# Linear attention: the last 32 low-rank rows of the gate as 96 stacked rows of one product

## The chip, the cores and the metric

The kernel runs on one core of a Trainium2 chip. The time is that of one execution on the device in microseconds; three runs of the kernel before gave 3934.86, 3940.90 and 3945.79, median 3940.9. A core has five engines with an instruction queue each: TensorE (PE, matrix products; its weight loads are listed as PEld), VectorE (DVE), ScalarE (ACT), GpSimd (POOL) and SyncE (SP, which here issues the loads). They wait for each other by semaphores alone.

## The reference

Two blocks of two layers each over 512 tokens of width 1024. The change lies in the first block, in the linear attention (an RWKV-7 time mix), and there in the gate `g`:

```python
zs = z + (shifted(z) - z) * mu
r, k, v, wd, ad, gd = split(zs, (1024, 1024, 1024, 64, 64, 160))
w = -softplus(-(w0 + tanh(wd) @ w2)) - 0.5      # decay
iclr = sigmoid(a0 + ad @ a2)                    # in-context rate
g = sigmoid(gd) @ g2                            # gate: 160 low-rank rows -> 1024
...
out = (groupnorm(scan(r, decay, k, v, ...)) + bonus) * g
```

The gate has 160 low-rank rows: a full tile of 128 and a rest of 32.

## The kernel before, in words

Activations are held transposed, channels on the partitions and 512 tokens along the columns. A product in full precision is made of three passes (`split_matmuls`, line 227): each factor is split into a high part, rounded to the format that PE takes at full rate, and a low part, what is left of it; high times high, high weight times low activation and low weight times high activation are summed in PSUM. Weights come as a stream of units, 128 rows by 1024 columns each, through two raw slots: SP loads a unit (`stream_loads`, L309), ACT writes its high part `Whi` (`HighParts`, L284), POOL its low part `Wlo` (`low_parts`, L299), both into one of three slots. PE takes unit u when the semaphore `w_lo` says that its low part is there.

The linear-attention stage first makes three low-rank tiles (decay and rate; the gate's first 128 rows; the gate's last 32 rows, the other 96 of that tile being zero), splits them into `loh` and `lol` (ACT L1327, DVE L1405), and then works through eight pairs of heads. A pair uses four units: r, k, L (all low-rank weights of the pair: decay, rate, gate 128 rows, gate rest) and v. `rwkv_lora_pe` takes unit L: six passes of 64 rows for decay and rate (L621), and the gate in two tiles of three passes each (through L232). The gate's second tile has 32 rows that count.

The order is written out by hand for each engine. For pair p, PE issues the scores (`rwkv_front_pe`, L709), then the low-rank products and the v product of pair p+1, then the five levels of a triangular inverse (`rwkv_inv_pe`, L719) with pieces of the r and k products of pair p+2 between them, then the tail (chunk states, output). The first pair's products stand before the loop. ACT evicts decay (wS, L885), rate (aS, L885) and gate (gS, L880), in that order, and then makes the high parts of the next r and k unit (L284). POOL multiplies the level masks (TM, L1146), and between the levels splits the next r and k unit in quarters of 256 columns (L299); in the tail it prepares b and k (L1099, L1101) and splits units L and v, in quarters as well. DVE masks the scores (L1124), forms the inverse's start (L1154 to L1159, the last being XT), scans the decay (L1048), mixes k (L1027, L1029, L1060: kkr) and adds up the levels (X L1166, XT L1168).

The output of pair p-1 is centred by DVE (L1216) in pair p, and the PSUM bank that its mean stands in is claimed again by PE for another product (`gv`) beside level 2 of the inverse: `claim` makes PE wait for L1216 there.

Of the kernel before, what the change touches and what calls it, by code (L numbers as in the profile page):

```python
# [18 lines left out]
F32 = mybir.dt.float32  # L19
# [6 lines left out]
ADD, SUB, MUL, MAX = ALU.add, ALU.subtract, ALU.mult, ALU.max  # L26

P = 128
# [8 lines left out]
LEAD = 2  # L37
PART = 8
GRING = 12
LOW_PIECES = 4  # L40
# [7 lines left out]
PAIRS = 8  # L48
# [178 lines left out]
def split_matmuls(pe, ps, left, right, n, start=True, stop=True):  # L227

    last = None
    for k in range(n):  # L230
        for i, (a, c) in enumerate(((0, 0), (0, 1), (1, 0))):
            last = pe.matmul(ps, left[a](k), right[c](k), start=start and k == 0 and i == 0,  # L232
                             stop=stop and k == n - 1 and i == 2)
    return last


def tiles_of(high, low):

    return (lambda k: high[:, k]), (lambda k: low[:, k])


def columns_of(unit, n, at=0, width=P, j=0, m=P):

    def part(x):
        w = x[:, at:at + n * width].rearrange("p (k n) -> p k n", k=n)
        return lambda k: w[:, k, j:j + m]
    return part(unit[0]), part(unit[1])


def weight_slot(b, u):  # L250
    return (u + b["slot0"]) % SLOTS


def raw_slot(b, u):
    return (u + b["raw0"]) % RAW
# [33 lines left out]
        self.upto(act, u + SLOTS)  # L289


def low_parts(pool, s, b, first, end, pieces=1):

    for u in range(max(first, LEAD), end):
        pool.wait_ge(s["w_hi"], u - LEAD + 1)
        slot = weight_slot(b, u)
        for i in range(pieces):
            part = slice(i * UNIT // pieces, (i + 1) * UNIT // pieces)
            last = pool.tensor_tensor(b["Wlo"][:, slot, part], b["raw"][:, raw_slot(b, u), part], b["Whi"][:, slot, part].bitcast(F32), SUB)  # L299
        last.then_inc(s["w_lo"], 1)  # L300


def stream_loads(sp, s, b, first, end, beside=None):

    for u in range(first, end):
        if u >= RAW + LEAD:
            sp.wait_ge(s["w_lo"], u - RAW - LEAD + 1)
        units, total = b["units"], b["units"].shape[0]
        sp.dma_start(b["raw"][:, raw_slot(b, u)], units[u] if u < total else b["next_units"][u - total]) \  # L309
            .then_inc(s[f"w_in{u % RAW}"], 16)  # L310
        if beside:
            beside(u)


def ada_load(sp, s, b, ada, layer, m):
# [119 lines left out]
def angle_sine(act, s, b, name, i, dst):  # L435
# [12 lines left out]
               first=("kkr", "c0", "c1", "c2", "c3", "cx", "big", "rn", "kk", "b", "kf", "ks", "na", "nr", "rk"))  # L448
# [17 lines left out]
POST_A = Steps("sq", "sd")  # L466
POST_V = Steps("d", "rr", "rw", "yn", "ya", "o", "og", "yh", "yl")

RWKV_SEMS = ["lo_hi", "lo_lo", "prep_g", "y_out", "lo_mm", "lo_z", "lo_d", "lo_mix", "lo_act", "gemm_p", "gemm_ev", "mix", "prep_v", "prep_a",
             "ssq_p", "front_p", "front_a", "front_v", "inv_g", "inv_p", "inv_a", "inv_v",  # L470
             "tail_p", "tail_a", "tail_v", "post_p", "post_a", "post_v", "bonus_p", "bonus_v"]

# [140 lines left out]
def rwkv_lora_pe(pe, s, b, ring, p):  # L613
    w = ring.take(pe)
    if p == 0:
        pe.wait_ge(s["lo_lo"], 3)
    banks = [claim(pe, s, b, "g", p, y) for y in "wa"]
    low = (b["loh"], b["lol"])
    for i, (a, c) in enumerate(((0, 0), (0, 1), (1, 0))):
        for h in range(2):  # L620
            last = pe.matmul(banks[h], w[a][half(h), h * P:(h + 1) * P], low[c][half(h), 0], start=i == 0, stop=i == 2)  # L621
            if i == 2:
                last.then_inc(s["gemm_p"], 1)
    ps = claim(pe, s, b, "g", p, "g")
    if p:
        pe.wait_ge(s["front_a"], FRONT_A(p - 1, "trV"))
    split_matmuls(pe, ps, columns_of(w, 2, at=2 * P), tiles_of(b["loh"][:, 1:3], b["lol"][:, 1:3]), 2).then_inc(s["gemm_p"], 1)


def head_sums(pe, ps, src, b):  # L630
# [239 lines left out]
def unit1(p, x):  # L870
    return 3 + 4 * p + ("rkLv" if p else "krLv").index(x)
# [523 lines left out]
def rwkv_dve(dve, s, b):  # L1395
    def mixed(i):
        dve.wait_ge(s["lo_z"], i + 1)
        dve.tensor_tensor(b["dz"][:, i], b["zp"][:, i, 0:TOK], b["zp"][:, i, 1:TOK + 1], SUB).then_inc(s["lo_d"], 1)
        dve.wait_ge(s["lo_d"], i + 1)
        dve.scalar_tensor_tensor(out=b["lo"][:, i], in0=b["dz"][:, i], scalar=b["p"]("mu", i),  # L1400
                                 in1=b["zp"][:, i, 1:TOK + 1], op0=MUL, op1=ADD).then_inc(s["lo_mix"], 1)

    def low(i):
        dve.wait_ge(s["lo_hi"], i + 1)
        dve.tensor_tensor(b["lol"][:, i], b["lo"][:, i], b["loh"][:, i].bitcast(F32), SUB).then_inc(s["lo_lo"], 1)  # L1405

    mixed(0)
    mixed(1)
    low(0)
    low(1)  # L1410
    mixed(2)
    low(2)
    rwkv_mix_dve(dve, s, b, 0, "k")
    rwkv_kk_dve(dve, s, b, 0)
    rwkv_mix_dve(dve, s, b, 0, "r")
    rwkv_scan_dve(dve, s, b, 0)
    rwkv_prep1_dve(dve, s, b, 0)
    rwkv_rn_dve(dve, s, b, 0)
    rwkv_prep2_dve(dve, s, b, 0)
    rwkv_prep3_dve(dve, s, b, 0)  # L1420
    rwkv_turned_dve(dve, s, b, 0)
    rwkv_mix_dve(dve, s, b, 0, "v")
    rwkv_prep4_dve(dve, s, b, 0)
    for p in range(PAIRS):
        rwkv_front_dve(dve, s, b, p)

        def between(l):
            if p + 1 < PAIRS and l == 0:
                rwkv_scan_dve(dve, s, b, p + 1)
                rwkv_mix_dve(dve, s, b, p + 1, "k")  # L1430
                rwkv_kk_dve(dve, s, b, p + 1)
            if l == 1 and p:
                rwkv_mean_dve(dve, s, b, p - 1)
            if p + 1 < PAIRS:
                if l == 1:
                    rwkv_prep1_dve(dve, s, b, p + 1)
                    rwkv_mix_dve(dve, s, b, p + 1, "r")
                if l == 2:
                    rwkv_mix_dve(dve, s, b, p + 1, "v")
                if l == 3:  # L1440
                    rwkv_rn_dve(dve, s, b, p + 1)
            if l == 4 and p:
                rwkv_rr_dve(dve, s, b, p - 1)
            if p + 1 < PAIRS:
                if l == 4:
                    rwkv_prep2_dve(dve, s, b, p + 1)
                if l == 5:
                    rwkv_turned_dve(dve, s, b, p + 1)
                    rwkv_prep3_dve(dve, s, b, p + 1)
            if l == 5:  # L1450
                rwkv_bonus_dve(dve, s, b, p)
        rwkv_inv_dve(dve, s, b, p, between)
        rwkv_tail_dve(dve, s, b, p)
    p = PAIRS - 1
    rwkv_mean_dve(dve, s, b, p)
    rwkv_rr_dve(dve, s, b, p)
    rwkv_out_dve(dve, s, b, p, ("yn", "ya", "o", "og", "yh", "yl"))


def rwkv_pool(pool, s, b):  # L1460
    low_parts(pool, s, b, 3, unit1(1, "L"))
    rwkv_prep_pool(pool, s, b, 0)
    low_parts(pool, s, b, unit1(1, "L"), unit1(2, "r"))
    for p in range(PAIRS):
        def between(l):
            if l in (1, 3):
                u = unit1(p + 2, "r" if l == 1 else "k")
                low_parts(pool, s, b, u, u + 1, LOW_PIECES)
            if p + 1 < PAIRS and l == 5:
                rwkv_prep_pool(pool, s, b, p + 1, "bk")  # L1470
            if l == 5:
                u = unit1(p + 2, "L")
                low_parts(pool, s, b, u, u + 2, LOW_PIECES)
        rwkv_inv_pool(pool, s, b, p, between)


# [1426 lines left out]
def ktiles(w, cols=slice(None)):  # L2903

    w = w[:, :, cols]
    return w.reshape(w.shape[0], -1, P, w.shape[2]).transpose(0, 2, 1, 3)


def rows_up(w, n=P):
    return np.concatenate([w, np.zeros((w.shape[0], n - w.shape[1], w.shape[2]), w.dtype)], 1)  # L2910


def layout1(a):
    L = LAYERS
# [5 lines left out]
    w = a["w_in"]  # L2920
    q0, k0, v0, r0, g0 = 0, 1024, 1280, 1536, 1536 + 3360
    rw = r0
    lo0 = rw + 3072
    def tile(m, c, k=slice(None)):

        return unit_of(ktiles(m, slice(c, c + P))[:, :, k])

    last = np.zeros((L, P, KD, P), np.float32)
    last[..., :32] = ktiles(w, slice(lo0 + 256, lo0 + 288))
    units = [tile(w, lo0), tile(w, lo0 + P), unit_of(last)]  # L2930
    wv = w[:, :, rw + 2048:rw + 3072][:, :, swap]
    g2 = a["rw_g2"][:, :, swap]
# [1 line left out]
    for p in range(PAIRS):  # L2934
        c = slice(p * P, p * P + P)
        of = {"r": tile(w, rw + p * P), "k": tile(w, rw + 1024 + p * P),
              "L": unit_of(np.concatenate([a["rw_w2"][:, :, c], none], 1), np.concatenate([none, a["rw_a2"][:, :, c]], 1),
                           g2[:, :P, c], rows_up(g2[:, P:, c])), "v": tile(wv, p * P)}
        units += [of[x] for x in ("rkLv" if p else "krLv")]
    wq = w[:, :, q0:q0 + 1024][:, :, qperm]  # L2940
    units += [tile(wq, P * i) for i in range(8)] + [tile(w, k0), tile(w, k0 + P), *[unit_of(ktiles(w, slice(v0, v0 + 256))[:, :, k:k + 4]) for k in (0, 4)]]
# [14 lines left out]
    stream = np.ascontiguousarray(np.stack(units, 1))  # L2956

    mu = a["rw_mu"]
    mu_lo = np.concatenate([mu[:, 3072:3360], np.zeros((L, 96), np.float32)], 1)
    mu_all = np.concatenate([mu_lo, mu[:, :2048], mu[:, 2048:3072][:, swap]], 1)  # L2960
    sink = a["att_sinks"][:, order].reshape(L, 8, 1, 2)
    sink = np.broadcast_to(sink, (L, 8, BLK, 2)).reshape(L, 1, 64)
# [208 lines left out]
```

## Time and profile before

| what | value |
|---|---|
| runs of the kernel before | 3934.86, 3940.90, 3945.79 us, median 3940.9 |
| profiled execution | span 3931.4 us from first to last instruction; the page gives no time around it |
| mean granted clock of PE | 0.979 |
| PE busy | 3743.9 us, 95% of the span, 30890 products |
| DVE, ACT, POOL busy | 1848.1, 1581.7, 1779.5 us |
| linear-attention stage | from the first low-rank tile at 39 us to the last output at 462 us in layer 1; the last output of layer 2 at 1721 us |

The page's busy time of PE counts each product from its start to its modelled end, and products overlap; what a product costs is read from the starts of those that follow each other. The list of waits says how long an engine stood still before a group of instructions, and for whom. The timeline gives start, duration, engine, line, operation, operands and, in brackets, the idle time before it and its releaser. Where several instructions of a line follow each other they are merged into one row (x4).

### The profile page before, as it was taken

The numbers are of one execution on the slowest core, as the hardware profiler recorded it, in microseconds if no ns is written. First come the engines' busy times: TensorE is split into PE (matmuls) and PEld (weight loads), VectorE is DVE, ScalarE is ACT, GpSimd is POOL, SyncE is SP. The second block draws the span as 40 slices with busy tenths as digits, with TensorE's granted clock in tenths as the row PEclk, the third lists the DMA queues.
The fourth block names the chain that finished last, engine by engine and source line by source line (L and its number), as shares of the span: only waits on it lengthen the run. The fifth ranks groups of instructions, "written<-read, shape, count | busy, mean of one in ns | idle before, by whom it ended". The sixth has DMA issues, their size and how long they took to land. (4 is left out here: it accounts for less than half of the span.)

```text
span 3931.4 us, 72626 instructions
## 1 busy us (share of the span) xinstructions
PE 3743.9 (95%) x30890; PEld 3040.7 (77%) x30904; DVE 1848.1 (47%) x2868; ACT 1581.7 (40%) x2643; POOL 1779.5 (45%) x1132
## 2 busy tenths in 40 slices
PE   7999989999998999998999999899999999999998
PEld 6777758878887777776887887677878877787887
DVE  7777652155635877754226553543231133423112
ACT  5555352343334555535234333454332234433222
POOL 5555444434445555544443444463444435344443
PEclk9999999989998999999998999899999999999999
DMA  4111203335532211122334553212222221222322
GB/s 142 52 56 56 88 28 135 99 134 193 183 107 76 92 51 56 56 99 72 99 105 143 189 182 104 69 65 76 97 86 97 97 85 66 70 96 87 97 97 86
DMA packets 108753, 379.88 MB, mean 97 GB/s; under 512 B 12560, under 2 KB 12944, under 8 KB 107792
## 3 DMA queue, kind: packets, MB, share of 16 engines
q1 hardware_dynamic: 102816, 365.66, 27.8%
q10 hardware_dynamic: 5616, 9.58, 0.7%
q8 instruction: 246, 4.03, 0.4%
q14 instruction: 75, 0.61, 0.1%
HBM read 359.46 MB, written 15.73 MB: 95 GB/s over the span
## 5 line engine op out<-in xcount | busy, mean ns | idle before, releaser
L299 POOL TENSOR_TENSOR Wlo<-raw,Whi 128x1024 fp32r<-128x1024 f32 (+1 forms) x744 | 1385.8, 1876 | 1671.6 <-ACT Whi L284 1671.4
L232 PE MATMUL ps<-hh,Whi 128*128 128x512 f32 x2864 | 1150.9, 402 | 22.1 <-DVE hl L383 10.1
L232 PE MATMUL ps<-hl,Whi 128*128 128x512 f32 x2864 | 1125.3, 393 | 0.0
L232 PE MATMUL ps<-hh,Wlo 128*128 128x512 f32 x2864 | 1124.4, 393 | 0.1
L284 ACT ACTIVATE Whi<-raw 128x1024 fp32r<-128x1024 f32 x552 | 578.7, 1054 | 689.3 <-PE ps L232 617.8
L232 PEld LDWEIGHTS ps<-hh,Whi 128*128 128x128 f32 x2864 | 543.3, 190 | 147.8 <-issue 15.7
L232 PEld LDWEIGHTS ps<-hh,Wlo 128*128 128x128 f32 x2864 | 543.0, 190 | 116.2 <-issue 0.5
L232 PEld LDWEIGHTS ps<-hl,Whi 128*128 128x128 f32 x2864 | 543.8, 190 | 108.1 <-issue 1.9
L232 PE MATMUL ps<-gh,Whi 128*128 128x512 f32 x864 | 337.9, 391 | 3.8 <-POOL Wlo L299 3.8
L232 PE MATMUL ps<-gh,Wlo 128*128 128x512 f32 x864 | 336.5, 390 | 0.0
L232 PE MATMUL ps<-gl,Whi 128*128 128x512 f32 x864 | 336.5, 389 | 0.0
L1146 POOL TENSOR_TENSOR TM<-TD,const 128x256 f32<-128x256 f32 x192 | 157.4, 843 | 152.3 <-PE ps L719 75.7
L1799 DVE TENSOR_TENSOR sg<-sg,ps 128x512 f32<-128x512 f32 x64 | 44.0, 688 | 366.9 <-PE ps L232 366.6
L232 PEld LDWEIGHTS ps<-gh,Whi 128*128 128x128 f32 x864 | 162.2, 188 | 39.0 <-POOL Wlo L299 5.5
L232 PEld LDWEIGHTS ps<-gh,Wlo 128*128 128x128 f32 x864 | 162.2, 188 | 33.8
L232 PEld LDWEIGHTS ps<-gl,Whi 128*128 128x128 f32 x864 | 162.3, 188 | 33.2
L2736 DVE SCALAR_TENSOR_TENSOR xT<-ps,mod,xT 128x512 f32<-128x512 f32 x64 | 48.1, 752 | 281.7 <-PE ps L232 281.7
L1992 ACT ACTIVATE acc<-ps,par 128x512 f32<-128x512 f32 x88 | 68.6, 780 | 273.5 <-PE ps L232 273.5
L2726 DVE TENSOR_TENSOR gt<-gt 128x512 f32<-128x512 f32 x64 | 47.9, 749 | 256.8 <-ACT gt L2614 256.8
L2043 DVE SCALAR_TENSOR_TENSOR acc<-ps,par,acc 128x511 f32<-128x511 f32 x88 | 66.0, 750 | 197.7 <-ACT acc L1992 197.7
L1782 ACT ACTIVATE sg<-ps 128x512 f32<-128x512 f32 x64 | 38.3, 599 | 239.2 <-PE ps L232 239.2
L719 PEld LDWEIGHTS ps<-X,TM 64*64 64x64 f32 x2560 | 81.8, 135 | 55.7 <-DVE y L1216 32.1
(365 smaller groups left out, 5652.8 us busy)
## 6 DMA issues: line engine op xcount, KB each, us to landing
raw<-in_stream SPq DMA_DIRECT2D x554, 512.0 KB, 3.3
ada<-in_ada SPq DMA_DIRECT2D x96, 512.0 KB, 4.3
park_x<-xT SPq DMA_DIRECT2D x2, 2048.0 KB, 7.3
park_yh<-yh ACTq DMA_DIRECT2D x16, 256.0 KB, 2.1
park_yl<-yl ACTq DMA_DIRECT2D x16, 256.0 KB, 2.5
xT<-park_x SPq DMA_DIRECT2D x2, 2048.0 KB, 8.3
yrh<-park_yh SPq DMA_DIRECT2D x16, 256.0 KB, 5.1
yrl<-park_yl SPq DMA_DIRECT2D x16, 256.0 KB, 4.9
```

The costliest lines, as they stand in the source:

```text
L232: last = pe.matmul(ps, left[a](k), right[c](k), start=start and k == 0 and i == 0, stop=stop and k == n - 1 and i == 2)
L284: act.activation(self.b["Whi"][:, weight_slot(self.b, u)], self.b["raw"][:, raw_slot(self.b, u)], ACT.Copy).then_inc(self.s["w_hi"], 1)
L299: last = pool.tensor_tensor(b["Wlo"][:, slot, part], b["raw"][:, raw_slot(b, u), part], b["Whi"][:, slot, part].bitcast(F32), SUB)
L719: return pe.matmul(b["ps"][half(u), bank, block(c)], left[:, block(c)], right[:, block(c)], start=True, stop=True)
L1146: pool.tensor_tensor(blocks(b["TM"][:, h, l % 2]), blocks(b["TD"][:, h]), lvl[:, l].broadcast_to([P, BLK, CB]), MUL) .then_inc(s["inv_g"], 1)
L1782: act.activation(b["sg"][:, i], b["ps"][:, i], ACT.Sigmoid).then_inc(s["gate_a"], 1)
L1799: dve.tensor_tensor(b["sg"][:, i], b["sg"][:, i], b["ps"][:, 4 + i], MUL).then_inc(s["gate_v"], 1)
L1992: act.activation(b["acc"][:, slot], b["ps"][:, slot], ACT.Identity, scale=b["p"]("cw2", j * FT + i), bias=b["p"]("cb", j * FT + i)).then_i ...
L2043: dve.scalar_tensor_tensor(out=b["acc"][:, slot, 1:TOK], in0=b["ps"][:, slot, 0:TOK - 1], scalar=b["p"]("cw1", j * FT + i), in1=b["acc"][: ...
L2726: dve.tensor_tensor(b["gt"][:, i % 4], b["gt"][:, i % 4], b["gt"][:, i % 4], MUL).then_inc(s["f1_v"], 1)
L2736: dve.scalar_tensor_tensor(out=b["xT"][:, m], in0=b["ps"][:, 4 + i % 3], scalar=b["mod"][:, 40 + m:41 + m], in1=b["xT"][:, m], op0=MUL, op ...
```

## The change

The gate's second tile takes one pass in place of three. The 32 rows are laid out three times: the weights of the low-rank tile's third unit (rows 0 to 31, 32 to 63, 64 to 95 of the result are equal), the mixing factors `mu`, and the rows of g2 in unit L. In the activation `loh`, DVE writes the low part over rows 32 to 63, where the high part was. In the weights `Whi`, POOL writes the low part over rows 64 to 95. One product over 96 rows then sums high times high, high weight times low activation and low weight times high activation.

```diff
+def stacked_low(pool, s, b, u):
+    slot, raw = weight_slot(b, u), raw_slot(b, u)
+    for part in (slice(0, 256), slice(256, 384)):
+        last = pool.tensor_tensor(b["Wlo"][:, slot, part], b["raw"][:, raw, part], b["Whi"][:, slot, part].bitcast(F32), SUB)
+    last.then_inc(s["rest_g"], 1)
+    pool.wait_ge(s["rest_g"], (u - unit1(0, "L")) // 4 + 1)
+    high = b["Whi"][REST_LOW, slot, REST]
+    pool.tensor_tensor(high, b["raw"][REST_LOW, raw, REST], high.bitcast(F32), SUB).then_inc(s["w_lo"], 1)
+    pool.wait_ge(s["w_lo"], u - LEAD + 1)
...
 def low_parts(...):
         pool.wait_ge(s["w_hi"], u - LEAD + 1)
+        if u in stacked:
+            stacked_low(pool, s, b, u)
+            continue
...
+GATE_REST = 32
+REST = slice(3 * P, 4 * P)
+REST_LOW = slice(2 * GATE_REST, 3 * GATE_REST)
...
 def rwkv_lora_pe(pe, s, b, ring, p):
-    split_matmuls(pe, ps, columns_of(w, 2, at=2 * P), tiles_of(b["loh"][:, 1:3], b["lol"][:, 1:3]), 2).then_inc(s["gemm_p"], 1)
+    split_matmuls(pe, ps, columns_of(w, 1, at=2 * P), tiles_of(b["loh"][:, 1:2], b["lol"][:, 1:2]), 1, stop=False)
+    rows = slice(0, 3 * GATE_REST)
+    pe.matmul(ps, w[0][rows, REST], b["loh"][rows, 2], start=False, stop=True).then_inc(s["gemm_p"], 1)
...
     def low(i):
         dve.wait_ge(s["lo_hi"], i + 1)
+        if i == 2:
+            amid = slice(GATE_REST, 2 * GATE_REST)
+            dve.tensor_tensor(b["loh"][amid, i], b["lo"][amid, i], b["loh"][amid, i].bitcast(F32), SUB).then_inc(s["lo_lo"], 1)
+            return
...
-    last[..., :32] = ktiles(w, slice(lo0 + 256, lo0 + 288))
+    for g in range(3):
+        last[..., 32 * g:32 * g + 32] = ktiles(w, slice(lo0 + 256, lo0 + 288))
...
-                           g2[:, :P, c], rows_up(g2[:, P:, c])), "v": tile(wv, p * P)}
+                           g2[:, :P, c], rows_up(np.concatenate([g2[:, P:, c]] * 3, 1))), "v": tile(wv, p * P)}
```

On PE, at the low-rank products of a pair (loh, lol: high and low part of the low-rank tiles; Whi, Wlo: of the weights), there stands before:

```order
L621 MATMUL ps<-loh,Whi 128x512 x2
L621 MATMUL ps<-lol,Whi 128x512 x2
L621 MATMUL ps<-loh,Wlo 128x512 x2
L232 MATMUL ps<-loh,Whi 128x512
L232 MATMUL ps<-lol,Whi 128x512
L232 MATMUL ps<-loh,Wlo 128x512
L232 MATMUL ps<-loh,Whi 128x512
L232 MATMUL ps<-lol,Whi 128x512
L232 MATMUL ps<-loh,Wlo 128x512
L232 MATMUL ps<-hh,Whi 128x512
```

And now, at the same place:

```order
L641 MATMUL ps<-loh,Whi 128x512 x2
L641 MATMUL ps<-lol,Whi 128x512 x2
L641 MATMUL ps<-loh,Wlo 128x512 x2
L232 MATMUL ps<-loh,Whi 128x512
L232 MATMUL ps<-lol,Whi 128x512
L232 MATMUL ps<-loh,Wlo 128x512
L649 MATMUL ps<-loh,Whi 128x512
L232 MATMUL ps<-hh,Whi 128x512
```

The second three passes of the gate are gone, and L649 is the one of 96 rows; the v product (hh) follows as before.

On POOL, in a pair's tail and into the next pair (kt, kh: prepared k; TM: level masks; Wlo in quarters of 256 columns, x8 being units L and v), there stands before:

```order
L1099 TENSOR_TENSOR kt<-dz,en 128x512
L1101 TENSOR_TENSOR kh<-kt,f 128x512
L299 TENSOR_TENSOR Wlo<-raw,Whi 128x256 x8
L1146 TENSOR_TENSOR TM<-TD,const 128x256 x4
L299 TENSOR_TENSOR Wlo<-raw,Whi 128x256 x4
```

And now:

```order
L1121 TENSOR_TENSOR kt<-dz,en 128x512
L1123 TENSOR_TENSOR kh<-kt,f 128x512
L296 TENSOR_TENSOR Wlo<-raw,Whi 128x256
L296 TENSOR_TENSOR Wlo<-raw,Whi 128x128
L300 TENSOR_TENSOR Whi<-raw,Whi 32x128
L314 TENSOR_TENSOR Wlo<-raw,Whi 128x256 x4
L1168 TENSOR_TENSOR TM<-TD,const 128x256 x4
L314 TENSOR_TENSOR Wlo<-raw,Whi 128x256 x4
```

Unit L's four quarters have become three instructions of 256, 128 and 128 columns; units v, r and k keep their quarters. For the units of pairs 0 and 1, which were split in one instruction of 1024 columns each, the same three stand in the place of L's one.

## Rows read from the trace of the kernel before

**Rows 1.** Waits of PE, whole span: line, waited for, us in total, times, longest.

```profile
PE ps L719 <- DVE y L1216: 27.0, 12, 2.3
...
PE ps L692 <- DVE v L1029: 1.4, 2, 0.8
...
PE ps L232 <- ACT wS L885: 0.4, 2, 0.2
```

**Rows 2.** Timeline of PE, the gate product of one pair: start, us, engine, line.

```profile
177.42 0.51 PE L232 MATMUL ps<-loh,Whi 128*128 128x512 f32 x1
...
178.69 0.39 PE L232 MATMUL ps<-loh,Wlo 128*128 128x512 f32 x1
178.92 0.40 PE L232 MATMUL ps<-hh,Whi 128*128 128x512 f32 x1
```

**Rows 3.** Timeline of PE, the same pair, around the wait for L1216.

```profile
189.37 0.39 PE L232 MATMUL ps<-hh,Wlo 128*128 128x512 f32 x1
192.00 0.27 PE L719 MATMUL ps<-X,TM 64*64 64x64 f32 x2 [2.24 <-DVE y L1216]
```

**Rows 4.** Timeline of DVE, the same pair, from the mask to L1216.

```profile
176.64 1.29 DVE L1124 TENSOR_TENSOR TK<-ps,const 128x512 f32<-128x512 f32 x2 [1.13 <-PE ps L709]
...
180.54 3.07 DVE L1159 TENSOR_TENSOR XT<-TM,const 64x256 f32<-64x256 f32 x4
...
189.17 0.85 DVE L1060 TENSOR_SCALAR kkr<-k,par 128x512 f32<-128x512 f32 x1
...
191.27 0.68 DVE L1216 SCALAR_TENSOR_TENSOR y<-ps,y 128x512 f32<-128x512 f32 x1
```

**Rows 5.** Timeline of all engines before the pair loop of layer 1.

```profile
74.60 5.59 POOL L299 TENSOR_TENSOR Wlo<-raw,Whi 128x1024 fp32r<-128x1024 f32 x2
75.22 2.75 DVE L1029 SCALAR_TENSOR_TENSOR v<-dz,par,zp 128x512 f32<-128x512 f32 x1
...
78.02 0.33 PE L692 MATMUL ps<-const,v 128*128 128x128 f32 x1 [0.63 <-DVE v L1029]
```

**Rows 6.** Timeline of POOL, a pair's tail.

```profile
214.26 5.56 POOL L299 TENSOR_TENSOR Wlo<-raw,Whi 128x256 fp32r<-128x256 f32 x8
224.87 0.74 POOL L1146 TENSOR_TENSOR TM<-TD,const 128x256 f32<-128x256 f32 x1 [5.05 <-ACT TD L944]
```

**Rows 7.** All XT instructions of DVE: duration in ns, min/median/max, first and last start.

```profile
L1159 DVE TENSOR_TENSOR XT<-TM,const x64: 420/850/876, 84.9 to 1684.6; 64x256 f32<-64x256 f32 x64
```

**Rows 8.** Timeline of ACT, the pair of rows 2: three evictions, two high parts.

```profile
177.52 0.69 ACT L885 ACTIVATE wS<-ps,par 128x512 f32<-128x512 f32 x1 [0.17 <-PE ps L621]
178.11 0.68 ACT L885 ACTIVATE aS<-ps,par 128x512 f32<-128x512 f32 x1
179.12 0.60 ACT L880 ACTIVATE gS<-ps 128x512 f32<-128x512 f32 x1 [0.33 <-PE ps L232]
179.62 2.00 ACT L284 ACTIVATE Whi<-raw 128x1024 fp32r<-128x1024 f32 x2
```

**Rows 9.** Waits of ACT for the gate product: us in total, times, longest.

```profile
ACT gS L880 <- PE ps L232: 3.7, 11, 0.3
```

**Rows 10.** Timeline of all engines, a stretch of 0.3 us: the first XT.

```profile
180.54 0.42 DVE L1159 TENSOR_TENSOR XT<-TM,const 64x256 f32<-64x256 f32 x1
...
180.74 0.82 POOL L299 TENSOR_TENSOR Wlo<-raw,Whi 128x256 fp32r<-128x256 f32 x1 [1.00 <-ACT Whi L284]
```

**Rows 11.** Windows: us, busy PE, PEld, DVE, ACT, POOL, granted clock, DMA, GB/s.

```profile
327.00:334.00 7.00, 7.00 (x150) 5.71 (x149) 6.87 (x9) 1.37 (x3) 7.00 (x9) 1.00 0.25 77
338.05:341.35 3.30, 3.30 (x68) 2.89 (x65) 3.16 (x7) 2.30 (x5) 1.56 (x2) 0.50 0.19 74
```

**Rows 12.** Timeline of DVE: L1216 of three pairs that follow each other.

```profile
287.78 0.68 DVE L1216 SCALAR_TENSOR_TENSOR y<-ps,y 128x512 f32<-128x512 f32 x1
...
336.00 0.68 DVE L1216 SCALAR_TENSOR_TENSOR y<-ps,y 128x512 f32<-128x512 f32 x1
...
385.79 0.68 DVE L1216 SCALAR_TENSOR_TENSOR y<-ps,y 128x512 f32<-128x512 f32 x1
```

More of the change, by code:

```diff
@@ L289, in around, with low_parts @@
         self.upto(act, u + SLOTS)
-def low_parts(pool, s, b, first, end, pieces=1):
+def stacked_low(pool, s, b, u):
[7 more added lines that the diff above has]
+    pool.wait_ge(s["w_lo"], u - LEAD + 1)
+def low_parts(pool, s, b, first, end, pieces=1, stacked=()):
     for u in range(max(first, LEAD), end):
         pool.wait_ge(s["w_hi"], u - LEAD + 1)
+        if u in stacked:
+            stacked_low(pool, s, b, u)
+            continue
         slot = weight_slot(b, u)
@@ L467 @@
 POST_V = Steps("d", "rr", "rw", "yn", "ya", "o", "og", "yh", "yl")
-RWKV_SEMS = ["lo_hi", "lo_lo", "prep_g", "y_out", "lo_mm", "lo_z", "lo_d", "lo_mix", "lo_act", "gemm_p", "gemm_ev", "mix", "prep_v", "prep_a",
+RWKV_SEMS = ["rest_g", "lo_hi", "lo_lo", "prep_g", "y_out", "lo_mm", "lo_z", "lo_d", "lo_mix", "lo_act", "gemm_p", "gemm_ev", "mix", "prep_v", "prep_a",
              "ssq_p", "front_p", "front_a", "front_v", "inv_g", "inv_p", "inv_a", "inv_v",
@@ L1460, in rwkv_pool @@
 def rwkv_pool(pool, s, b):
-    low_parts(pool, s, b, 3, unit1(1, "L"))
+    low_rank = [unit1(p, "L") for p in range(PAIRS)]
+    low_parts(pool, s, b, 3, unit1(1, "L"), stacked=low_rank)
     rwkv_prep_pool(pool, s, b, 0)
-    low_parts(pool, s, b, unit1(1, "L"), unit1(2, "r"))
+    low_parts(pool, s, b, unit1(1, "L"), unit1(2, "r"), stacked=low_rank)
     for p in range(PAIRS):
@@ L1472, in between @@
                 u = unit1(p + 2, "L")
-                low_parts(pool, s, b, u, u + 2, LOW_PIECES)
+                low_parts(pool, s, b, u, u + 2, LOW_PIECES, low_rank)
         rwkv_inv_pool(pool, s, b, p, between)
@@ L2958, in layout1 @@
     mu = a["rw_mu"]
-    mu_lo = np.concatenate([mu[:, 3072:3360], np.zeros((L, 96), np.float32)], 1)
+    mu_lo = np.concatenate([mu[:, 3072:3360], mu[:, 3328:3360], mu[:, 3328:3360], np.zeros((L, 32), np.float32)], 1)
     mu_all = np.concatenate([mu_lo, mu[:, :2048], mu[:, 2048:3072][:, swap]], 1)
```

## The prediction

> **What bounds the kernel now.** I read the waits of TensorE (PE) first, then the stretch around the changed product on every engine that touches it, then the chain from there to the next place where PE stops, and the granted clock last. The change touches only the linear-attention stage of the two layers of the first block, so the waits of PE in that stage decide. The reader is to see that by far the longest one there is not for weights and not for a product: twelve times, 27.0 us in all, PE stops in front of the third level of the triangular inverse until VectorE (DVE) has written the centred output of the pair before (L1216) [rows 1]. That is once for each of the pairs 1 to 6 of each layer.
>
> The pair shown starts its gate product at 177.42 and is through with it when the value product begins at 178.92 [rows 2]. PE then runs without a gap until its last product issued at 189.37, stands 2.24 us, and goes on at 192.00 [rows 3]. What it stands for is a chain that DVE works through without a pause from the mask at 176.64 to L1216, which starts at 191.27 and takes 0.68, so ends at 191.95 [rows 4]. The mask was released by the scores, which PE issues before the low-rank products. So the stage is bound by DVE from the mask to L1216, and the changed product lies beside that chain, not on it.
>
> **The change, part by part.**
>
> PE, the gate product. Six passes become four, in sixteen places (eight pairs, two layers). A busy duration of 0.39 us a pass is not its price: passes overlap, and the next one starts 0.23 us after the one at 178.69 [rows 2]. Two passes are 0.46 us, 32 of them 7.4 us. That is the largest gain there is to have. I take a pass over 96 rows at the same 0.23; if the change of height costs what the first pass of a product shows, the saving is smaller by 0.1, and it cannot be more than 0.46.
>
> Where the 0.46 goes. In the twelve pairs with the wait on L1216, PE arrives 0.46 earlier at a wait that ends at the same time: 2.24 becomes 2.70 and nothing is gained. In pair 0 of each layer the value product after the gate's already waits for ScalarE's eviction of the decay gate (0.4 us in two times) [rows 1], which needs nothing of the gate's last passes: no gain there either. That leaves the first product of each layer, made before the pair loop, where PE has no wait until it transposes v. There it stands 1.4 us in two times [rows 1], 0.63 in layer 1 [rows 5] and so 0.77 in layer 2.
>
> GpSimd (POOL), the low parts of the low-rank unit. A unit of 1024 columns becomes 256 + 128 columns over all rows and 128 columns over 32 rows, so 512 columns in three instructions, with two waits for its own results. In the pair loop this lies in the tail: eight quarters (two units) take 5.56 us from 214.26, 0.70 each, and POOL then idles 5.05 us [rows 6]. Four quarters become three shorter ones, at most 1.4 us saved, hidden by that idle time; the two added waits are not in the trace, and even at 1 us each they would fit into it. Queued behind them on POOL is the v unit, which PE wants only after its low-rank products, so nobody waits for it. SyncE's loads that these results release go out earlier; PE's waits on loads are not among those of this stage.
>
> At the start of a layer it is another matter. POOL's whole-unit subtractions from 74.60 (5.59 us for the low-rank and the v unit of pair 1) overlap DVE's v at 75.22, which takes 2.75 us, and PE stands for just that v [rows 5]. The median of DVE's other short operations is far lower: an XT is 0.42 at least and 0.85 in the median [rows 7]. I read it as DVE held up by POOL's instruction and let go when it ends. Cut into short instructions, the low-rank unit lets v in early, and PE's 0.63 and 0.77 go, together with the 0.46 in front of them. What is late next is DVE's mask, which needs the scores and so moves with PE. Gain: 0.46 + 0.63 + 0.46 + 0.77 = 2.3 us. From below it is 0, if something else holds PE there.
>
> DVE and ScalarE. The low part of the third low-rank tile goes from 128 to 32 rows at the same 512 columns; durations follow the columns, so I take no gain. Evictions keep their number and shape. The doubled and tripled weights and mixing factors are data prepared before the launch and change no instruction.
>
> What the earlier gate product sets off. This is the part that I think decides. ScalarE's queue is: decay gate at 177.52, in-context rate at 178.11, then the gate's eviction at 179.12 after 0.33 us of waiting for the product, then two high parts from 179.62 [rows 8]; eleven of the sixteen gate evictions wait like that, 3.7 us in all [rows 9]. With the product done 0.46 earlier, the eviction can start right behind the one before it: 0.59 after 178.11, so at 178.70, or when that ends, at 178.79. The high part, and with it POOL's first low part of the next r unit, comes 0.33 to 0.42 earlier. That low part started at 180.74, 0.20 us after DVE's first XT at 180.54, and that XT took only 0.42 [rows 10]. From there the two engines alternate: four XTs take 3.07 [rows 4], so the three after the first cost 0.88 each, one POOL instruction and one of DVE in turn, until POOL's twelve instructions are through.
>
> With the change POOL starts at 180.32 to 180.41, ahead of the XT. The first XT then waits for POOL's instruction (about 0.70) and ends 0.28 after it (that is how long after POOL's end the second XT ended before: 180.54 + 0.42 + 0.88 = 181.84 against 180.74 + 0.82 = 181.56). So: first XT ends at 180.32 + 0.70 + 0.28 = 181.30 to 181.39, the second 0.88 later at 182.18 to 182.27 instead of 181.84. DVE is 0.34 to 0.43 later, because one more of POOL's instructions goes first, and stays so through the alternation until kkr (0.85 at 189.17, a TENSOR_SCALAR) [rows 4]. L1216 and PE's restart are 0.38 later in eleven pairs: 11 x 0.38 = 4.2 us. From both sides: had POOL not passed the XT, DVE could gain the 0.20 by which the two stand apart; had it passed it by a hair, DVE would lose 0.88 - 0.28 = 0.6. So -2.2 to +6.6 for eleven.
>
> The Trainium skill, SBUF — State Buffer, section "SBUF: two separate sides", says that VectorE (with two SBUF inputs) and GpSimd share a port pair as an exclusive lock: whoever starts first keeps it for its whole instruction. The trace's 0.42 and 0.85 for the same XT agree [rows 7]. By that rule an earlier POOL instruction is a loss for DVE, which speaks against this change; by a share of bandwidth instead, the order of the two would not matter and the sum would lack the 4.2.
>
> The clock. PE's wait grows from 2.24 to 2.24 + 0.46 + 0.38 = 3.1 us. After three of the twelve waits the granted clock is at 0.50 (1.2 instead of 2.4 GHz), one of them at 338.05 to 341.35 [rows 11]; PE had stood before it. That pair took 385.79 - 336.00 = 49.79 against 336.00 - 287.78 = 48.22 [rows 12]: 1.57 us a time. Longer waits should bring more of these. Bounds: none more (0) and all twelve (9 x 1.57 = 14.1); I take three more, 4.7, nearer to the three in twelve that the rows show than to twelve.
>
> Sum: -2.3 + 0 + 4.2 + 4.7 = +6.6 us on the profiled span of 3931.4. The page gives no time around that span; it is 9.5 below the median of the three runs and 3.5 below the fastest. I put the change on the median: 3940.9 + 6.6, some 3947 us, +0.16%. A measurement of this kernel can tell about 0.3% (11.8 us) from no change, so this is a forecast of no change that can be measured.
>
> **The rivals.**
>
> A, the saving is simply hidden: POOL doesn't pass the XT, or DVE makes it up before L1216. For it: L1216 waits for the last of several products too; against it: the margin of 0.20 is less than the 0.33 by which ScalarE can move up. Then only the start counts: 3940.9 - 2.3 = 3939.
>
> B, the whole saving arrives: 7.4 + 1.4 = 8.8 us, 3932. It needs DVE's chain to shorten too; DVE shows no pause in it, and nothing of the chain is removed. If a pass were worth its busy 0.39, 32 of them would be 12.5 and just measurable; the spacing of 0.23 speaks against that.
>
> C, slower beyond the bound: the longer wait brings the half clock after nearly every pair. Mechanism: PE's wait in front of the third level, 3.1 us; price 1.57 a time; with all nine others -2.3 + 4.2 + 14.1 = +16.0, so 3957. It decides from seven more on (7 x 1.57 + 1.9 = 12.9 over 11.8). Against it, nine waits of 2.24 passed without. The Trainium skill, TensorE: Matmul & The Clock Gate, section "Why this matters for your kernels", warns that idle gaps between bursts of matmuls put TensorE back to the half clock; three of twelve waits here agree, nine don't, and by the rule the longer wait would be C.
>
> D, the change doesn't do what it says: the 96-row pass, or the wait of POOL for itself, costs more than the two passes. Two waits and a change of height would have to add over 0.46 on PE's path; then 3941 to 3948, not to be told from the forecast.
>
> **How the numbers follow.** Forecast (POOL passes the XT, some more half clock; 3940 to 3953): 0.56. A: 0.20. B: 0.07. C: 0.14. D: 0.03. From 3934 to 3957 leaves out most of B and half of C, and a median of three that itself moves by some 4 us. Slower by over 0.3%: nearly all of C and a tenth of the forecast, 0.19. Faster by over 0.3%: a part of B and a mishap, 0.05. Within: 0.76.
>
> **What would show it.** In the changed kernel's trace: the wait of PE on the DVE line of L1216 grows from 27.0 to about 37 us in twelve (A and the forecast differ here: 32.5 against 37); the gate eviction follows the rate's without waiting; POOL's first quarter starts before the first XT, and that XT takes about 0.85 instead of 0.42; the period of a pair without half clock goes from 48.22 to about 48.6; the waits of PE for v are gone; stretches at 0.50 in the stage number about six. I am wrong if the period falls, if the first XT stays at 0.42, or if the wait grows by no more than 0.46 a pair.

## The result and the profile after

The changed kernel takes 3951.35 us (median of 8 runs, 3946.53 to 3956.45) against 3939.65 of before (8 runs beside them): a ratio of 1.0034, 95% interval 1.0025 to 1.0043. That is slower by about the 0.3% that was called measurable. The medians lie 11.7 us apart where 6.6 were forecast, and the time is 4 us above the predicted 3947. The profiled spans differ by 3946.5 - 3931.4 = 15.1 us. Lines after the low-rank code stand 22 lower in the changed kernel: L1216 is now L1238, L719 L741, L1159 L1181, L299 L314.

The waits of PE, the whole span (line, waited for, us in total, times, longest):

```profile
PE ps L741 <- DVE y L1238: 36.6, 12, 3.1
...
PE ps L860 <- issue: 3.8, 1, 3.8
PE ps L232 <- ACT wS L907: 1.8, 2, 0.9
```

The wait of [rows 1] is still the largest in the stage and has grown from 27.0 to 36.6, 0.80 a time. The wait for v is gone; that for wS in pair 0 took up the shorter passes, 0.4 to 1.8. New is a stop of 3.85 us, once, in the last pair of layer 1, in which PE waits for nothing that the profile shows ("issue").

The timeline of the pair of rows 2, 8 and 10, PE, ACT, POOL and DVE:

```profile
177.56 0.39 PE L232 MATMUL ps<-loh,Wlo 128*128 128x512 f32 x1
177.68 0.68 ACT L907 ACTIVATE aS<-ps,par 128x512 f32<-128x512 f32 x1
177.79 0.40 PE L649 MATMUL ps<-loh,Whi 96*128 96x512 f32 x1
178.03 0.40 PE L232 MATMUL ps<-hh,Whi 128*128 128x512 f32 x1
178.25 0.60 ACT L902 ACTIVATE gS<-ps 128x512 f32<-128x512 f32 x1
178.73 2.01 ACT L284 ACTIVATE Whi<-raw 128x1024 fp32r<-128x1024 f32 x2
...
179.88 0.75 POOL L314 TENSOR_TENSOR Wlo<-raw,Whi 128x256 fp32r<-128x256 f32 x1 [0.53 <-ACT Whi L284]
180.13 0.77 DVE L1181 TENSOR_TENSOR XT<-TM,const 64x256 f32<-64x256 f32 x1
```

The 96-row pass (L649) is followed by the next one after 0.24 us, as a pass over 128 rows is after 0.23 [rows 2]. The gate's eviction no longer waits [rows 8]. POOL's quarter now starts 0.25 us ahead of the first XT, where it stood 0.20 behind it [rows 10], and that XT takes 0.77 in place of 0.42. The same order stands in all twelve pairs.

The end of the same pair, DVE and PE, and ahead of it the L1238 of one period earlier:

```profile
142.59 0.68 DVE L1238 SCALAR_TENSOR_TENSOR y<-ps,y 128x512 f32<-128x512 f32 x1
...
191.19 0.68 DVE L1238 SCALAR_TENSOR_TENSOR y<-ps,y 128x512 f32<-128x512 f32 x1
191.92 0.27 PE L741 MATMUL ps<-X,TM 64*64 64x64 f32 x2 [3.06 <-DVE y L1238]
```

From the first XT to L1238 it was 10.73 us (180.54 to 191.27, [rows 4]); now it is 11.06, and the period without half clock is 191.19 - 142.59 = 48.60 in place of 48.22 to 48.26.

Windows of the granted clock (columns as in rows 11): before the restart of PE in this pair, behind it, and behind the "issue" stop:

```profile
188.90:192.90 4.00, 0.98 (x64) 0.98 (x64) 3.96 (x9) 2.90 (x5) 1.83 (x3) 1.00 0.32 100
193.00:196.20 3.20, 3.20 (x75) 2.81 (x68) 3.02 (x7) 2.47 (x6) 1.80 (x2) 0.50 0.09 29
463.10:469.00 5.90, 5.90 (x21) 3.30 (x21) 3.44 (x7) 0.59 (x1) 0.00 (x0) 0.50 0.02 6
```

The clock falls to 0.50 (1.2 GHz) behind eight of the twelve waits; before it was three. A ninth stretch follows the "issue" stop.

The start of layer 1, PE, POOL and DVE, against [rows 5]; first the first low-rank product and the first XT of the kernel before, then the changed kernel:

```profile
55.91 0.50 PE L621 MATMUL ps<-loh,Whi 64*128 64x512 f32 x2
...
84.92 0.42 DVE L1159 TENSOR_TENSOR XT<-TM,const 64x256 f32<-64x256 f32 x1
```

```profile
56.20 0.50 PE L641 MATMUL ps<-loh,Whi 64*128 64x512 f32 x2
...
74.69 2.05 POOL L296 TENSOR_TENSOR Wlo<-raw,Whi 128x256 fp32r<-128x256 f32 x2
75.31 1.11 DVE L1051 SCALAR_TENSOR_TENSOR v<-dz,par,zp 128x512 f32<-128x512 f32 x1
...
79.60 1.29 DVE L1146 TENSOR_TENSOR TK<-ps,const 128x512 f32<-128x512 f32 x2 [2.32 <-PE ps L731]
...
81.64 0.42 DVE L1150 TENSOR_TENSOR TB<-ps,const 128x256 f32<-128x256 f32 x1 [0.38 <-ACT TD L966]
...
84.09 1.34 DVE L1181 TENSOR_TENSOR XT<-TM,const 64x256 f32<-64x256 f32 x2
```

v takes 1.11 instead of 2.75, and the mask starts at 79.60 instead of 80.66. ScalarE's TD takes part of that back (DVE waits 0.38 for it, 0.19 before): the first XT is at 84.09 instead of 84.92. The low-rank products began 0.29 later in this execution (56.20 for 55.91), ahead of all that the change touches. From their first to the first XT it is 27.89 for 29.01, a gain of 1.1; in layer 2 it is 27.89 for 29.14, so 1.25.

The 15.1 us of the profiled spans, by the starts of L1216 and L1238:

| stretch | us | what it is |
|---|---|---|
| up to the first of layer 1 | -0.45 | start of layer 1: -1.1, and 0.3 for the later begin, so -0.83 to the first XT; then 0.4 of the new order |
| first to seventh of each layer | +10.56 | ten periods, 0.35 each, 3.5 of the new order; five more half-clock stretches, 8.1 (the eight cost 12.7, the three of before 4.5); less 1.1 for two pairs of before in layer 2 (48.48 and 49.13) that were longer without half clock |
| tail of layer 1 (39.36 for 32.47) | +6.9 | the "issue" stop, 3.85, and the half clock behind it |
| between the layers, start of layer 2 | -1.9 | start of layer 2, -1.25, then 0.4 of the new order; the rest in stages that the change doesn't touch |

### The profile page after: what moved, and what is told of

Its sections match the earlier page's. It is cut to its first block and busy times, and to the rows that moved or that the text cites. A ratio compares the mean times of both kernels' runs of the same rounds, so it can differ in the third digit from the quotient of the medians.

```text
span 3946.5 us, 72574 instructions
## 1 busy us (share of the span) xinstructions
PE 3744.0 (95%) x30858; PEld 3040.5 (77%) x30872; DVE 1844.2 (47%) x2868; ACT 1582.7 (40%) x2643; POOL 1765.7 (45%) x1128
## 5 line engine op out<-in xcount | busy, mean ns | idle before, releaser
L314 POOL TENSOR_TENSOR Wlo<-raw,Whi 128x1024 fp32r<-128x1024 f32 (+1 forms) x692 | 1343.3, 1952 | 1670.6 <-ACT Whi L284 1669.5
L232 PE MATMUL ps<-hh,Whi 128*128 128x512 f32 x2864 | 1151.8, 402 | 24.3 <-DVE hl L406 10.3
L741 PEld LDWEIGHTS ps<-X,TM 64*64 64x64 f32 x2560 | 83.7, 137 | 65.2 <-DVE y L1238 41.6
```

Of the source, the lines that this page charges most:

```text
L741: return pe.matmul(b["ps"][half(u), bank, block(c)], left[:, block(c)], right[:, block(c)], start=True, stop=True)
```

## The experiments

Theory when they began: the change does nothing but end the gate's product earlier; ScalarE, and so POOL, move up; POOL's quarter gets in front of DVE's XT; the longer wait of PE costs clock. Rival: the 96-row pass, or POOL's added waits, cost it. The ratios are to the kernel before, timed beside each kernel; each kernel ran 4 to 12 times, and its trace shows one execution. Periods are without half clock.

**Two passes less, by leaving them out** (part of the computation is missing: the correction passes of the 32 rows; POOL's and DVE's work is that of before):

```diff
-    split_matmuls(pe, ps, columns_of(w, 2, at=2 * P), tiles_of(b["loh"][:, 1:3], b["lol"][:, 1:3]), 2).then_inc(s["gemm_p"], 1)
+    split_matmuls(pe, ps, columns_of(w, 1, at=2 * P), tiles_of(b["loh"][:, 1:2], b["lol"][:, 1:2]), 1, stop=False)
+    pe.matmul(ps, w[0][:, 3 * P:4 * P], b["loh"][:, 2], start=False, stop=True).then_inc(s["gemm_p"], 1)
```

> The kernel before without two of the six gate passes (the two correction passes of the last 32 rows are left out); no 96-row pass, no added waits of POOL, its low parts as before. Theory: slower all the same, like the change: the wait on L1216 about 36.5 us in twelve, first XT about 0.77, period 48.6, eight or so stretches at half clock in the stage, ratio 1.003 to 1.005 (the change's gain at the start of a layer lacks). Rival 1 (96-row pass or added waits): not slower, 0.998 to 1.000. Rival 2 (clock alone): wait 32.5 us, first XT 0.42, period 48.25 without half clock, ratio 1.001 to 1.003.

Measured 1.0043 (1.0029 to 1.0056): as slow as the change, without its 96-row pass and its POOL code. Waits of PE and the timeline around the first XT:

```profile
PE ps L720 <- DVE y L1217: 35.3, 12, 3.1
PE ps L839 <- issue: 3.6, 1, 3.6
PE ps L693 <- DVE v L1030: 1.8, 2, 0.9
```

```profile
180.51 3.39 POOL L299 TENSOR_TENSOR Wlo<-raw,Whi 128x256 fp32r<-128x256 f32 x4 [0.53 <-ACT Whi L284]
180.78 2.52 DVE L1160 TENSOR_TENSOR XT<-TM,const 64x256 f32<-64x256 f32 x3
```

POOL is ahead of the XT, the period is 48.6, seven half-clock stretches. The rival falls. It is a control for the layer's start as well: POOL's unit is long here, v takes 2.75, and the wait for it is there (1.8). The low-rank products and the first XT:

```profile
56.12 0.49 PE L621 MATMUL ps<-loh,Whi 64*128 64x512 f32 x2
...
84.92 0.42 DVE L1160 TENSOR_TENSOR XT<-TM,const 64x256 f32<-64x256 f32 x1
```

From the one to the other it is 28.80, against 29.01 before and 27.89 with the change. So 0.2 of the 1.1 at the start come with the passes, and the other 0.9 with the rest of the change, in which v, beside POOL's shorter unit, takes 1.11.

**The high parts first** (before, ScalarE makes the next two high parts ahead of the gate's eviction):

```diff
-            rwkv_ev_act(act, s, b, p + 1, "wag")
+            rwkv_ev_act(act, s, b, p + 1, "wa")
         high.upto(act, unit1(p + 2, "k") + 1)
+        if p + 1 < PAIRS:
+            rwkv_ev_act(act, s, b, p + 1, "g")
```

> The kernel before, with one edit: ScalarE makes the next two high parts ahead of the gate's eviction, so POOL's first quarter can start some 0.4 us earlier while PE's work is untouched. Theory (POOL passes DVE's first XT): the first XT takes about 0.77 us instead of 0.42, the wait of PE on L1216 goes from 27.0 to about 31 us in twelve (0.32 more each), the period of a pair without half clock from 48.25 to about 48.57; with a few more stretches at half clock the ratio to before is 1.001 to 1.003. Rival 1 (the 96-row pass or POOL's added waits cost the time): no change, 1.000. Rival 2 (the longer idle time of PE by itself, through the clock): no change, since PE's work is the same.

A miss: 0.9979 (0.9971 to 0.9988), faster. POOL and the first XT:

```profile
179.40 0.85 POOL L299 TENSOR_TENSOR Wlo<-raw,Whi 128x256 fp32r<-128x256 f32 x1
...
180.15 0.42 DVE L1159 TENSOR_TENSOR XT<-TM,const 64x256 f32<-64x256 f32 x1
```

POOL starts 0.75 ahead of the XT, so its first quarter is nearly through when the XT comes, and the second starts 0.05 behind it: the XT takes 0.42. The period is 47.80. So "POOL earlier" is not a loss as such: what counts is where POOL's instruction lies against DVE's. The reading of the trace that explains the whole gain came with the next kernel.

**The change, with the high parts first**, the same edit on the kernel after:

> The kernel after, with ScalarE making the high parts of the next r and k unit ahead of the gate's eviction (the same edit on the kernel before ran at 0.9979). Here the gate product's end no longer decides when GpSimd starts. Theory: GpSimd's first quarter starts 0.75 us ahead of the first XT, as in that kernel, XT 0.42, L1216 10.2 behind it, period 47.8: the loss of 0.34 a pair that the change brings is gone. TensorE's wait for L1216 is 22.2 + 12 x 0.46 = 27 to 28 us in twelve, so one to four half-clock stretches at 1.5 us, and the stall of about 3 us in layer 1's last pair is there. Ratio 0.9980 to 0.9995. Rival (the change makes VectorE's chain longer by something other than that order): period 48.1 to 48.2, 1.0005 to 1.0020.

1.0021 (1.0012 to 1.0031), above the expected range: the period is 48.23, as the rival had it, POOL again 0.75 ahead and the XT 0.42. The timelines tell the two kernels apart, first before with the edit, then after with it, POOL and DVE behind the XTs:

```profile
182.90 1.73 POOL L1146 TENSOR_TENSOR TM<-TD,const 128x256 f32<-128x256 f32 x2
183.25 2.79 DVE L1048 TENSOR_TENSOR_SCAN cum<-const,wS 128x128 f32<-128x128 f32 x4
184.85 1.73 POOL L1146 TENSOR_TENSOR TM<-TD,const 128x256 f32<-128x256 f32 x2 [0.21 <-PE ps L719]
```

```profile
183.59 3.35 POOL L1168 TENSOR_TENSOR TM<-TD,const 128x256 f32<-128x256 f32 x4
183.94 3.28 DVE L1070 TENSOR_TENSOR_SCAN cum<-const,wS 128x128 f32<-128x128 f32 x4
```

In the first, POOL's third mask waits 0.21 us for PE's level-1 product; one scan goes through alone and the four take 2.79. In the second PE is earlier by the passes saved (this product comes 3.44 behind the first XT, in the first kernel 3.92), POOL doesn't wait, and the scans take 3.28: 0.49 more, the difference from the first XT to L1216 (10.23, 10.72). The periods differ by 0.43 (47.80, 48.23). With this order of ScalarE's the change makes POOL early in a second place. Nine stretches at half clock where one to four were expected (PE's wait is 2.7 each) and the "issue" stop (2.5) do the rest.

**PE's wait filled** (after; twelve products whose result nobody reads, into a free bank, in front of the wait, pairs 1 to 6), and the same with eight on the kernel before:

```diff
+            if l == 1 and 1 <= p < PAIRS - 1:
+                for i in range(12):
+                    pe.matmul(b["ps"][:, 2], b["loh"][:, 0, 0:P], b["loh"][:, 1], start=True, stop=True)
```

> The changed kernel, with twelve products of 512 columns into a free PSUM bank put in front of PE's wait on L1216 in pairs 1 to 6 (2.7 us of the 3.1 us wait; nothing reads them). Theory: the wait falls from 36.6 to about 5 us, the half-clock stretches behind it go, every pair takes 48.6, ratio to before 1.0000 to 1.0015: what is left is twelve times 0.32 less the start of the layers. Rival 1: no change against the changed kernel, 1.0034. Rival 2 (clock alone): all of the loss goes, 0.998 to 0.9995.

> The kernel before, with eight products of 512 columns (into a bank that is free there) in the wait of TensorE for L1216, pairs 1 to 6. They take 8 x 0.23 = 1.8 of the 2.24 us. Theory (a half-clock stretch follows the standing of TensorE there and costs 1.5 us): the three stretches of before are gone, the periods are all 48.25, the time 3 x 1.5 = 4.5 us less: ratio 0.9980 to 0.9995. Rival (the stretches come without regard to that wait): as many as before, 0.9995 to 1.0010.

The filled kernel after: 0.9989 (0.9980 to 0.9998), lower than expected. Its wait for L1238:

```profile
PE ps L741 <- DVE y L1238: 3.8, 12, 0.3
```

There is no half clock behind it, the "issue" stop is gone too (0.2 left, tail of layer 1 32.46), and the period is still 48.61. The ratio alone lies in the range of rival 2; what speaks against that rival is the period, from which none of the 0.35 of the new order went. My expectation had forgotten that the three stretches of before go as well, and that the number of products ahead of the stop changes. From after to this one 1.0034 - 0.9989 = 0.45%, some 18 us, went: by the trace the eight stretches (12.7) and the stop with its half clock (6.9), while the stages between the layers took 3.2 longer in this execution. The filled kernel before: 0.9991 (0.9982 to 1.0000), no stretch behind the twelve waits, 3.3 us less for three; its ratio could be the rival's as well, its trace not. So the half clock follows PE's standing there, and filling the wait takes it away while the order stays.

**Two short products in front of the gate product** (after; PE's program has again as many products as before):

```diff
+    for i in range(2):
+        pe.matmul(ps[:, 0:64], b["loh"][:, 1, 0:P], b["loh"][:, 1, 0:64], start=True, stop=True)
     split_matmuls(pe, ps, columns_of(w, 1, at=2 * P), ...
```

> The kernel after, with two products of 64 columns put in front of each gate product (the result of the gate overwrites theirs), so that TensorE's program has as many products as before. In the traces of the three kernels that have 32 products fewer (after, the one without two of the six gate passes, and the one in which GpSimd waits), TensorE stands 2.8 to 3.9 us between the same two instructions of the last pair of layer 1, each time the 8450th of its program, and a 16 KB packet of the instruction queue falls into it; the kernels with another count show nothing there. Theory (the stall goes with the place of that instruction in the program): it is gone here, the tail of the last pair of layer 1 falls from 39.4 to about 33-35 us. The two short products give about 0.1 us of the 0.46 back, GpSimd's first quarter starts some 0.15 us ahead of the first XT instead of 0.26, which is still ahead, so the period stays 48.6 and the half-clock stretches stay near eight. Ratio to before 1.0018 to 1.0030. Rival (the stall is chance, or comes from the longer waits before it): it is here as well, 1.0030 to 1.0040.

1.0023 (1.0015 to 1.0032), in the expected range. PE's waits show no "issue" stop in layer 1, whose tail is 32.48 again; seven stretches. The four kernels with 32 products fewer than before all have the stop at the same instruction of PE's program, the 8128th product; of those with another count one has it too, as the last experiment shows. In the stretch from 458.5 to 463.5 of after one packet of the instruction queue (q8) moved, 16 KB:

```profile
q8 instruction: 1, 0.02, 1.2%
```

Such packets come all along the trace, 246 of them, so one row says little. The starts say more: in the five traces with the stop PE goes on 2.39 to 2.45 us after the start of that packet (460.63 and 463.03 here), whether it stood 1.44 or 3.85; in the seven others the 8128th product starts 2.77 to 4.04 after the last such packet, without a stop. That fits a PE that stands for its instructions; no run moved the packet alone. One thing was not as expected: POOL stands only 0.05 ahead of the XT, and that is the worst place:

```profile
181.62 1.62 POOL L314 TENSOR_TENSOR Wlo<-raw,Whi 128x256 fp32r<-128x256 f32 x2 [0.74 <-ACT Whi L284]
181.67 1.85 DVE L1183 TENSOR_TENSOR XT<-TM,const 64x256 f32<-64x256 f32 x2
```

The first XT takes 0.96 and the period is 48.76, longer than the change's own.

**Eight short products there**, the same edit with eight:

> The kernel after, with eight products of 64 columns in front of each gate product instead of the two passes that went (their result is overwritten). They take about 0.4 to 0.5 us by the two of the run before (two moved GpSimd's start by 0.2). Theory (the order of GpSimd and VectorE hangs on when the gate's product ends, and nothing else in the change): GpSimd's first quarter starts 0.15 to 0.3 us behind the first XT as before the change, XT 0.42, L1216 10.73 behind it, period 48.25; TensorE's wait 2.2 to 2.3 each, two to four half-clock stretches instead of eight; no stall of 3 us in layer 1's last pair, since the count of products is another. The 0.8 us at each layer's start stay: ratio 0.9990 to 1.0005. Rival (GpSimd's shorter low-rank unit or the 96-row pass lengthens VectorE's chain): period 48.5 or more, 1.0015 to 1.0030.

0.9974 (0.9964 to 0.9983): faster than before, and better than expected. The eight cost 0.87 (0.11 each, not the 0.05 to 0.06 I had assumed), so the gate product, passes saved and all, ends later than it did before the change. POOL is 0.60 behind:

```profile
181.25 2.64 DVE L1183 TENSOR_TENSOR XT<-TM,const 64x256 f32<-64x256 f32 x4
181.85 2.63 POOL L314 TENSOR_TENSOR Wlo<-raw,Whi 128x256 fp32r<-128x256 f32 x3 [1.40 <-ACT Whi L284]
```

Two XTs pass at 0.42, the four take 2.64 instead of 3.07, the period is 47.81, PE's wait 17.3 in twelve, no half clock is left in the pairs, and the "issue" stop isn't there. The shorter low-rank unit and the 96-row pass are in this kernel, so the rival falls here too. Work that is of no use, in front of the product that the change made shorter, gains 0.6% (1.0034 - 0.9974), some 24 us, over the change.

**POOL made to wait for the XTs** (after, and before with the same edit):

```diff
                 u = unit1(p + 2, "r" if l == 1 else "k")
+                if l == 1:
+                    pool.wait_ge(s["inv_v"], INV_V(p, "T01"))
```

> The changed kernel, with POOL waiting for the last of DVE's four XTs before it starts the low parts of the next r unit. Theory: the four XTs take about 1.8 us instead of 3.4, L1216 ends about 1.9 us earlier in a pair than in the changed kernel, the wait on it falls from 36.6 to 10 to 18 us in twelve, no half clock behind it, the period goes to about 46.6; ratio to before 0.992 to 0.996. Rival 1: ratio stays above 1.001. Rival 2 (clock alone): wait shorter only by what the order gives, ratio about 0.9995.

> The kernel before, with GpSimd waiting for the second half's XT of level 1 before it splits the next r unit (the same wait as in the kernel after that ran at 0.9936). Theory (the change takes nothing off the path in the twelve pairs; what it cost was the order of GpSimd and VectorE, and the clock): the same order as in that kernel, XT 0.42, L1216 9.0 us behind the first XT, period 46.6, TensorE's wait for L1216 about 0.6 to 0.7 each (1.1 less the 0.46 that the gate product still takes); so the change is worth nothing in the pairs here either, and the two differ by the start of the layers (this one some 0.8 to 1.6 us longer) and by the stall of 2.8 us that this one doesn't have: ratio to before 0.9925 to 0.9945. Rival (with the order mended, the four passes of the gate are a saving on the path, 0.3 to 0.46 a pair): 0.9950 to 0.9975, period above 46.9.

After with it: 0.9936 (0.9923 to 0.9948). Before with it: 0.9926 (0.9913 to 0.9938). The timeline of the first:

```profile
176.03 1.78 DVE L1181 TENSOR_TENSOR XT<-TM,const 64x256 f32<-64x256 f32 x4
177.89 3.33 POOL L314 TENSOR_TENSOR Wlo<-raw,Whi 128x256 fp32r<-128x256 f32 x4 [2.65 <-DVE XT L1181]
```

Four XTs take 1.78 for 3.07, and the first scan, which POOL's first quarter now follows too, 0.42 for 0.85. The period is 46.5 to 46.6 in most pairs of both kernels, and there is no half clock behind the wait, which is, after and before:

```profile
PE ps L741 <- DVE y L1238: 12.4, 12, 1.1
```

```profile
PE ps L719 <- DVE y L1216: 6.8, 12, 0.9
```

With the order mended the change still takes nothing off a pair: the two have the same period, and PE's wait is 6.8 in twelve without the change and 12.4 with it, 0.47 a time, the passes saved.

**Both mended** (after, POOL waiting, and the two short products):

> The kernel after in which GpSimd waits for XT (0.9936), with the two short products in front of each gate product as well. Theory (the stall goes with the place in the program): the stall of 2.8 us in layer 1's last pair is gone, the pairs as they were (period 46.6, the short products in front of a wait), ratio 0.9925 to 0.9935. Rival (the stall is chance): no lower than 0.9936.

0.9916 (0.9903 to 0.9929), the fastest of all, 3903.37 us, a little under the expected range, with which the interval overlaps. The "issue" stop in layer 1's last pair is not gone, as the theory had it, but shorter, and a second one of 1.3 stands at the start of layer 2's pairs. The first:

```profile
PE ps L847 <- issue: 1.4, 1, 1.4
```

It is again at the 8128th product, which is now another line; the tail of layer 1 is 34.27, against 36.83 without the two short products and 32.47 without a stop. So the number of products ahead does not decide by itself: the kernel before has as many and doesn't stop. The interval also overlaps that of the kernel before with POOL waiting, so whether the change is worth its 1.1 us at a layer's start there can't be told.

POOL's first quarter against the first XT, as in most pairs of seven of the kernels (two further columns: mean wait of PE for the centred output, half-clock stretches behind the twelve):

| kernel | POOL behind (+) or ahead (-) | XT to L1216 | period | wait | stretches |
|---|---|---|---|---|---|
| after, POOL waits | +1.86 | 9.01 | 46.55 | 1.03 | 0 |
| after, eight short products | +0.60 | 10.30 | 47.81 | 1.44 | 0 |
| before | +0.20 | 10.73 | 48.25 | 2.25 | 3 |
| after, two short products | -0.05 | 11.24 | 48.76 | 2.90 | 7 |
| after | -0.25 | 11.06 | 48.60 | 3.05 | 8 |
| after, high parts first | -0.75 | 10.72 | 48.23 | 2.72 | 9 |
| before, high parts first | -0.75 | 10.23 | 47.80 | 1.85 | 1 |

## Why the prediction was near, and where it was wrong

The mechanism was right. DVE's chain bounds the pair, and the two passes went into PE's wait (0.47 a time). POOL got in front of the XT, the XT got longer, and the wait came out at 36.6 against the "about 37" forecast. The period came out at 48.6, as forecast.

The start of the layers: v's wait went, for the reason given (POOL's long unit; with two passes less and that unit left long it stays). 1.1 and 1.25 us were gained for the 2.3 of the sum. The size is in part luck: that ScalarE's TD is late next and takes 0.2 back was not named, but the mask had come 1.35 earlier in layer 1, counted from the first low-rank product, where the sum has 1.09.

DVE's chain: 0.35 in twelve pairs, 4.2 us, for 0.38 in eleven, 4.2. The bound of 0.6, had POOL passed "by a hair", was nearly reached by the kernel with POOL 0.05 ahead: 0.51. The other bound, a gain of 0.20, missed the cases of POOL far ahead or well behind. The Trainium skill, SBUF — State Buffer, section "SBUF: two separate sides", says that the one that starts first holds the shared ports for its whole instruction. The traces agree: the first XT takes 0.42 when POOL starts 0.20 behind it, and when POOL is ahead it takes what is left of POOL's instruction and the 0.28 of the prediction, 0.75 - 0.25 + 0.28 = 0.78 (measured 0.77) and 0.74 - 0.05 + 0.28 = 0.97 (measured 0.96).

The clock is the term that was too small. It said "I take three more, 4.7, nearer to the three in twelve that the rows show than to twelve". Five more came, 8.1 us. The price was right (1.6 each for 1.57), the number was not. The runs give the relation it lacked: mean waits of up to 1.44 us left no stretch in twelve, 1.85 one (behind a wait of 2.02), 2.25 three, 2.7 and more seven to nine. From 2.7 on the count doesn't follow the length (nine at 2.72, eight at 3.05), and behind the stops that wait for nothing it is less regular still: none behind 2.5 in the change with the high parts first, 6.8 us of half clock behind 1.3 in the last kernel. Five lies between the three of the sum and the nine of rival C.

What the sum lacked altogether is the "issue" stop in the last pair of layer 1, 6.9 us with the half clock behind it. It is not on the path that the prediction followed: it came with a PE program 32 products shorter, and two idle products in front of each gate product took it away. Without it the profiled spans would differ by 8.2 us, 0.21%, and the kernel with the product count restored measured 0.23% (0.15 to 0.32), though with a longer period: by these numbers the forecast of no change that can be measured held for the gate, and the stop carried the time to the bound. That 3951 lies even within the forecast's own 3940 to 3953 is in part luck: in the profiled spans the clock and the stop are 10.3 us more than the sum has, while the medians, by which the forecast went, came out only 5.1 further apart than forecast.

## What to carry to other kernels

A product that lies beside the bounding chain has consumers, and making it earlier makes them earlier too: look for the place where one of them meets an instruction of the bounding engine that it can hold up, and work out both sides of the meeting from the starts, since a shift of 0.45 us against the other engine cost 0.35 a pair here while an ordering wait at that place gained 1.7. A wait of PE that grows is not free when it is already followed by half clock now and then. And when a small edit brings a stop that waits for nothing, count the instructions ahead of it and look for a packet of the instruction queue in front of its end: two idle products took this one away in one kernel, and left half of it in another.

## What was not expected of the hardware

- The cost of POOL beside DVE is not steady in POOL's start: 0.60 behind 10.30 us, 0.20 behind 10.73, 0.05 ahead 11.24, 0.25 ahead 11.06, 0.75 ahead 10.72 with the change and 10.23 without.
- PE stopped for 1.4 to 3.9 us between two neighbouring products of one line, in five kernels at the same place of its program, with no semaphore to wait for, and went on 2.4 us after a 16 KB packet of the instruction queue had started.
- Eight products of 64 columns between products of 512 took 0.11 us each; a pass over 96 rows 0.24, like one over 128.
